# Layer 0's output projection with half its inputs by pairs of rows

## What is computed

```
y = jnp.concatenate([ya * jax.nn.silu(ga), yb * jax.nn.silu(gb)], axis=-1)
return y @ w_out            # layer 0: (1024 x 2048) @ (2048 x 1024)
...
x = x + gate[:, None, :] * y
```

## Time and profile before

| | |
|---|---|
| median of 3 runs | 1289.84 us (1289.24 to 1289.9) |
| the profiled execution | 1291.17 us |
| its span | 1289.4 us |
| TensorE busy | 1269.2 us, 98% |
| VectorE, ScalarE, GpSimd busy | 984.4, 641.3, 320.2 us |
| DMA | 167.31 MB, mean 130 GB/s |

### The profile page before, as it was taken

One profiled execution on the slowest core, in us unless ns is written; L12 is line 12 of the kernel. 1 busy time (PEld: TensorE's weight loads), 2 busy tenths in 40 slices (PEclk: granted clock), 3 DMA queues, 4 the chain that ended last, 5 costly groups with the idle time before them and its releaser, 6 DMA issues.

```text
span 1289.4 us, 15493 instructions
## 1 busy us (share of the span) xinstructions
PE 1269.2 (98%) x5655; PEld 1047.7 (81%) x5655; DVE 984.4 (76%) x1148; ACT 641.3 (50%) x904; POOL 320.2 (25%) x187
## 2 busy tenths in 40 slices
PE   7999999999999999999999999999999999999997
PEld 6877888888888888888888888888888888888886
DVE  5899997878878886868467599848748747797677
ACT  7456656465646464635558464234233333443353
POOL 1043443433424343000000013132223121413200
PEclk8999999999999999999999999999999999999999
DMA  9712232323242332597847302232232232782053
GB/s 303 210 49 70 84 118 86 104 81 114 65 120 70 114 107 74 172 386 268 305 155 271 113 17 66 69 96 65 68 96 67 66 98 82 287 284 65 18 179 132
DMA packets 151507, 167.31 MB, mean 130 GB/s; under 512 B 6342, under 2 KB 125318, under 8 KB 151432
## 3 DMA queue, kind: packets, MB, share of 16 engines
q1 hardware_dynamic: 151432, 166.33, 40.2%
HBM read 141.14 MB, written 25.17 MB: 129 GB/s over the span
## 4 chain that ended last, share of the span: by engine, by line
PE 86%; DVE 10%; SPq 2%; issue 2%; DMA 1%; ACT 0%; DVEq 0%; ACTq 0%
PE psum L2401 28%; PE psum L2403 28%; PE psum L2402 28%; DVE w_lo L1546 1%; DVE X L2320 1%; SPq L631 1%; DVE whole_x L2003 1%; DVE X L1636 1%; DVE y_lo L1613 1%; PE psum L2548 1%; DMA late<-in_mod_w 1%; SPq L644 0%; SPq L620 0%; DVE bufs L1785 0%; DVE w_lo L1568 0%
## 5 line engine op out<-in xcount | busy, mean ns | idle before, releaser
L2401 PE MATMUL psum<-X,w_hi 128*128 128x512 f32 x1252 | 490.3, 392 | 1.8 <-DVE w_lo L1546 0.9
L2402 PE MATMUL psum<-X,w_hi 128*128 128x512 f32 x1252 | 488.4, 390 | 0.0
L2403 PE MATMUL psum<-X,w_lo 128*128 128x512 f32 x1252 | 488.1, 390 | 0.0
L2401 PEld LDWEIGHTS psum<-X,w_hi 128*128 128x128 f32 x1252 | 235.7, 188 | 53.1 <-issue 2.7
L2403 PEld LDWEIGHTS psum<-X,w_lo 128*128 128x128 f32 x1252 | 235.7, 188 | 49.3
L2402 PEld LDWEIGHTS psum<-X,w_hi 128*128 128x128 f32 x1252 | 235.8, 188 | 48.9 <-issue 0.2
L999 ACT ACTIVATE w_hi<-ssum 128x512 fp32r<-128x512 f32 x156 | 97.1, 626 | 143.4 <-PE psum L2403 111.7
L1546 DVE TENSOR_TENSOR w_lo<-raw,w_hi 128x1024 fp32r<-128x1024 f32 x82 | 102.9, 1256 | 79.1 <-ACT w_hi L977 78.8
L928 POOL TENSOR_TENSOR ssum<-raw 128x512 f32<-128x512 f32 x39 | 73.6, 1886 | 311.2 <-DMA raw<-in_pool_w_in 253.1
L1568 DVE TENSOR_TENSOR w_lo<-ssum,w_hi 128x512 fp32r<-128x512 f32 x156 | 131.2, 849 | 25.6 <-ACT w_hi L999 25.0
L936 POOL TENSOR_TENSOR ssum<-ssum,raw 128x512 f32<-128x512 f32 x39 | 61.3, 1571 | 340.5 <-DVE w_lo L1568 340.5
(11 more groups left out here) (277 smaller groups left out, 1996.2 us busy)
## 6 DMA issues: line engine op xcount, KB each, us to landing
raw<-in_hy_w_in SPq DMA_DIRECT2D x48, 512.0 KB, 5.2
raw<-in_hy_w_out SPq DMA_DIRECT2D x48, 512.0 KB, 5.0
raw<-in_pool_w_in SPq DMA_DIRECT2D x32, 512.0 KB, 5.1
aux<-in_mod_w SPq DMA_DIRECT2D x16, 512.0 KB, 4.0
y_dram<-bufs SPq DMA_DIRECT2D x16, 512.0 KB, 2.9
raw<-in_mod_w SPq DMA_DIRECT2D x16, 512.0 KB, 5.2
y_dram<-gb_ SPq DMA_DIRECT2D x16, 512.0 KB, 3.3
raw<-in_pool_w_out SPq DMA_DIRECT2D x16, 512.0 KB, 6.0
```

The lines of the kernel that those rows point to most:

```text
L2401: nc.tensor.matmul(out_, whi, xhi, start=first, stop=False, skip_group_check=check)
L2402: nc.tensor.matmul(out_, whi, xlo, start=False, stop=False, skip_group_check=check)
L2403: return nc.tensor.matmul(out_, wlo, xhi, start=False, stop=last, skip_group_check=check)
```

## The change

Layer 0's output projection gets the form that layer 1's has. Input blocks 0 to 7 go by passes of 8 steps, A over rows 0 to 3, B over 4 and 5, C over 6 and 7. Input blocks 8 to 15 go by four pairs of row blocks ("O0"), between passes A and B. The other edits follow from it:

- the weights of blocks 8 to 15 are loaded into whole_x in pass A by `out_weights(0, kp)`, and GpSimd, VectorE and ScalarE make and split their T sums there;
- the 16 loads of the modulation leave the ring; each now goes to one of two rows of bufs (`mod_rows`), and the additions stand between the pairs' instructions on VectorE (`MODS_OF`: 4, 5, 5, 2 in the four pairs);
- y of passes B and C is loaded, 256 columns wide, to other places (`y_narrow`), as are the rows of x and their products with the gate;
- the gate's sums come behind product 7 of the first pair, the column sums in four pieces between the four parts of step 1 of pass B; the turns are groups of four, two and two row blocks;
- GpSimd starts its first T sums of layer 0 when the operand "ga" is split.

```diff
 PAIRS = [(name, i) for i in range(1, HEADS) for name in "ABC"]
+PAIRS += [("O0", j) for j in range(SB // 2)]
 PAIRS += [(name, n) for n in range(GROUPS) for name in ("V01", "G01", "V23", "G23") if n or name[1] == "2"]
-PAIRS += [("O", j) for j in range(SB // 2)]
+PAIRS += [("O1", j) for j in range(SB // 2)]
...
-N_STEPS = (2 * KB, KB)
-BLOCKS = {(0, "A"): (0, 1, 2), (0, "B"): (3, 4, 5), (0, "C"): (6, 7), (1, "A"): (0, 1, 2, 3), (1, "B"): (4, 5, 6, 7)}
+N_STEPS = (KB, KB)
+BLOCKS = {(0, "A"): (0, 1, 2, 3), (0, "B"): (4, 5), (0, "C"): (6, 7), (1, "A"): (0, 1, 2, 3), (1, "B"): (4, 5, 6, 7)}
...
+MODS_OF = (range(0, 4), range(4, 9), range(9, 14), range(14, 16))
...
+            def mod_load(m):
+                if m < 2:
+                    sp.wait_ge(ylo_done, KB)
+                else:
+                    sp.wait_ge(mod_done, m - 1)
+                _, chunk, kk = mods1[m]
+                sp.dma_start(mod_rows(m), mod_w[1][kk * P:(kk + 1) * P, chunk * D:(chunk + 1) * D])\
+                  .then_inc(mod_in[m % 2], 16)
+            def out_weights(layer, kp):
+                sp.wait_ge(full_of["4"], OUT[layer])
...
+            for n, step in enumerate(s for s in STEPS if s[:2] == (0, "A")):
                 ring_load(("W",) + step)
                 y_load(step)
+                if n in (1, 2):
+                    for kp in (2 * n - 2, 2 * n - 1):
+                        out_weights(0, kp)
+                if n in (3, 4):
+                    spill_head(HEADS - 1, n - 3)
+                if n >= 4:
+                    rows_load(0, n - 4)
+            for k in PAIRED[0]:
+                sp.wait_ge(y_out[k], 16)
+            o0 = OUT[0]
+            pair_load(o0)
+            pair_load(o0 + 1)
+            bias_load(1)
+            for m in (0, 1):
+                mod_load(m)
+            for b in (4, 5):
+                rows_load(0, b)
+            for m in (2, 3):
+                mod_load(m)
...
-            pool.wait_ge(h_ready, KB)
+            pool.wait_ge(lo_done, HI["ga", 0])
...
+            for n in range(3, KB):
+                step_splits(steps_a[n])
+                if n >= 4:
+                    low_out(0, n - 4)
+                if n < 7:
+                    t2_and_t4_out(0, n - 3)
...
+            for j, q in enumerate(OUT_PAIRS[0]):
+                mods = list(MODS_OF[j])
+                if j:
+                    take_22(q - 1)
+                    prep(q, 0)
...
+                add_11(q)
+                for m in mods[:2] if j < 3 else ():
+                    add_mod(m)
+                prep(q, 4)
+                for m in mods[2:4] if j < 3 else ():
+                    add_mod(m)
+                prep(q, 5)
...
+                add_12(q)
+                for m in mods[4:] if j < 3 else ():
+                    add_mod(m)
+                prep(q, 6)
```

More of the change, by code:

```diff
@@ L216, in build @@
         for n, (_, p, k) in enumerate(s for s in STEPS if s[0] == layer):
-            if (layer, p, k) == (1, "B", GROUP_ORDER[0]):
-                for q in range(OUT, len(PAIRS)):
+            if p == "B" and n == KB:
+                for q in OUT_PAIRS[layer]:
                     add_pair(q)
@@ L424, in build @@
         gate_in = sem("gate_in")
+        mod_in = [sem(f"mod_in{n}") for n in range(2)]
         y_out = [sem(f"y_out{k}") for k in range(2 * KB)]
@@ new lines, in _ @@
+            rows_store(1)
+            for m in (7, 8):
+                mod_load(m)
+            pair_load(o0 + 3)
+            for m in (9, 10):
+                mod_load(m)
+            rows_store(2)
+            mod_load(11)
+            rows_store(3)
+            rows_load(0, 7)
+            for m in (12, 13):
+                mod_load(m)
+            for step in STEPS[KB:KB + 2]:
+                ring_load(("W",) + step)
+            for m in (14, 15):
+                mod_load(m)
+            rows_load(0, 6)
@@ L818, in _ @@
+            for n, step in enumerate(s for s in STEPS if s[0] == 0 and s[1] != "A"):
+                if n >= 2:
+                    ring_load(("W",) + step)
+                y_load(step)
+                if n in (KB + 3, KB + 4):
+                    rows_store(n - KB + 1)
             for name in ("V0", "V1", "G0", "G1"):
@@ L1342, in _, with upper_out @@
-            passes(0, 3)
+                half = first // HALF
+                cols = slice(first - half * HALF, last - half * HALF)
+                nc.scalar.activation(h_half(k, half, 0)[:, cols], hx(k)[:, first:last], ACT.Copy)\
+                  .then_inc(hhi_ready, 1)
+            def upper_out(layer, kp):
+                at = 2 * ((2 * layer + 1) * KP + kp) + 2
+                act.wait_ge(t24_added, at)
+                act.wait_ge(t13_added, at)
+                for blocks in (slice(0, 4), slice(4, 7)):
+                    nc.scalar.activation(X[:, kp, blocks, 0, :], whole_x[kp][:, blocks, 1, :], ACT.Copy).then_inc(out_hi, 1)
@@ L1997, in residual @@
                     at = o_count(layer, b, half)
-                    if (layer, half) == (0, 0) and b >= 4:
-                        dve.wait_ge(*full(("T", b // 4 - 1 if b < 7 else 1, KB - 1)))
                     if (layer, b, half) == (1, 0, 0):
@@ L2108, in _ @@
             inverse(0, 7)
+            for k in range(KB):
+                low_h1(1, k)
             for k in range(KB):
@@ new lines, in _ @@
+                if p == "B":
+                    first = OUT[layer]
+                    for q in OUT_PAIRS[layer]:
+                        pair(q, after_1=(lambda: last_of(q - 1)) if q > first else None,
+                             after_7=gate_sums if q == OUT[0] else None)
+                for n, y_step in enumerate(y_steps[:ends]):
+                    if (layer, p, n) == (0, "A", 0):
+                        operands(y_step)
+                        for b, half in ((0, 0), (0, 1), (1, 0), (1, 1), (2, 0)):
+                            part_of(y_step, b, half)
+                        last_of(Q["C", HEADS - 1])
+                        part_of(y_step, 2, 1)
+                        operands(y_steps[1])
+                        for half in range(2):
+                            part_of(y_steps[1], 0, half)
+                        for half in range(2):
+                            part_of(y_step, 3, half)
+                        continue
+                    if (layer, p, n) != (0, "A", 1):
+                        operands(y_step)
+                    for b in blocks[1:] if (layer, p, n) == (0, "A", 1) else blocks:
+                        for half in range(2):
+                            if p == "B" and (n, b, half) == (0, 5, 1):
+                                last_of(OUT_PAIRS[layer][-1])
@@ L2787, in _ @@
                             part_of(y_step, b, half)
+                            if (layer, p, n) == (0, "B", 1):
+                                sums_between(2 * blocks.index(b) + half)
                     behind(layer, p, n)
```

610 lines of the change are left out of this document (319 added, 291 removed).

## The result

The changed kernel takes **1320.6 us** (median; 1319.3 to 1322.9), the kernel before, on the same chip, 1290.2: ratio **1.0233**, 95% interval 1.0221 to 1.0245. It is slower by 30.4 us, where 18.0 were forecast and the range ended at 1317. The sign was right, the size too small. The profiled execution took 1322.9 us (span 1321.1); before it was 1291.17 (span 1289.4).

The account below looks back on a forecast made before the run. TensorE, busy 98% of the span, was taken to bound the kernel, if operands arrive. Terms: -13.4 saved, +18.3 +1.6 in pass A, +9.9 +1.6 in the pairs: +18.0 on 1289.84, so 1307.8 us; range 1294 to 1317.

Parts of the forecast that it names:

- Clock behind the column sums, 1.6 us: Modulation sums in four pieces: the clock holds for the eight matmuls behind them, 1.6 us saved.
- GpSimd's start, 0.9 us: Layer 0's first GpSimd sums start one operand split later, so TensorE's wait for that split shortens: 0.9 us saved.
- Pass A, loads: Output-weight loads queue ahead of steps 2 and 3; step 3's weights land at T+19.2, T being product 4's end.
- Rival (a): Pass A's load queue is faster than layer 1's: step 3's weights at T+16.8, 2.4 us earlier, time 1305.4; chance 0.12.
- Pass A, chain and clock, 18.3 + 1.6: VectorE's fixed order of work makes step 7 late: 18.3 us lost, plus 1.6 for slow clock behind the last wait.
- The 8 us of the bound: Pass A's lower bound: with loads for nothing, VectorE's chain starts near 538.5 and still ends 8 us late.
- rival (c): Faster: step 3's operands come earliest, pass A loses only 8 us and the pairs nothing, 1284.4; chance 0.07.
- Pairs, 9.9 + 1.6 us: Product 4 waits for VectorE in the second and third pairs: 9.9 us lost, plus 1.6 for the clock.
- Passes B and C, 0: ScalarE and VectorE keep up with the 2.72 us steps, cover about 0.4 us a step: nothing lost.
- Rival (d): VectorE worse off: GpSimd contention in every pair, 5.2 us loads, slow clock behind four waits; +30, 1320; chance 0.09.
- Rival (b): Only pass A waits; in the pairs the additions' loads land in time as VectorE catches up: 1296.3; chance 0.22.
- Under 13 us of waits: Sign of being wrong: TensorE's waits between 526 and V0's start sum to under 13 us.

Follow-up runs that it names:

- run 6: The kernel before with only the column sums cut into four pieces between parts of step 6 of pass B: 1289.5 us, ratio 0.9988.
- run 7: The changed kernel with GpSimd's first sums of layer 0 starting again as in the kernel before: 1320.5 us.
- run 1: The changed kernel with the eight output-weight loads issued behind the loads of steps 2 and 3 instead of ahead: 1315.95 us, ratio 1.0203.
- run 2: The changed kernel loading only the first two of sixteen modulation rows, with all sixteen additions kept: 1308.4 us.
- run 3: The changed kernel loading only two modulation rows, and with fourteen of sixteen additions cut to 16 of 1024 columns: 1301.6 us.
- Run 5: The changed kernel with matmuls of a zero matrix filling TensorE's waits in pass A and the pairs: 1320.8 us, ratio 1.0232.
- run 8: The changed kernel with output-weight loads later, additions respaced 4, 5, 4, 3, GpSimd's first-pair sums delayed, its old start restored, norms apart: 1312.9 us.

## Why the prediction was right in sign and too small

By its own steps, in spans; the stages add up to what is missing (1.1 + 1.6 + 8.5 + 2.6 = 13.8 of 31.7 - 18.0 = 13.7):

- **48 matmuls, 10.9 us:** right. 48 fewer stand on the page, and layer 1 is unchanged.
- **Clock behind the column sums, 1.6 us:** right; run 6 measured 1.55 (0.5 to 2.7).
- **GpSimd's start, 0.9 us:** wrong. The wait moved from 71 to 96 us, and pass A begins 0.2 us later rather than 0.9 earlier: 1.1 us missing. The profiles of the runs, with the same work up to there but for GpSimd's start, have pass A begin between 525.5 and 528.3, so its start alone cannot show 0.9 us; the two waits of run 7 do. The step took a wait's end for a gain without asking who is late next.
- **Pass A, loads:** right. The weights of step 3 had landed at 551.1, where ScalarE's wait for them ends; product 4 ended at 532.9, so at T+18.2 (forecast T+19.2).

```profile
551.13 1.06 ACT L1048 ACTIVATE w_hi<-raw 128x1024 fp32r<-128x1024 f32 x1 [2.95 <-DMA raw<-in_hy_w_out]
```

By the estimate from the Trainium skill (DMA: Bandwidth & Descriptors, "Anatomy of one DMA") it would have been T+14.6; the measurement is 3.6 us later. The section gives that sum for one transfer issued by GpSimd, and here eleven were queued by SyncE, which the prediction did not say. Rival (a), T+16.8, is 1.4 us off, the forecast 1.0 the other way.
- **Pass A, chain and clock, 18.3 + 1.6:** nearly right. Measured, the pass ends at 594.6 instead of 592.8 (1.6 more from its own start). The 2.1 us of GpSimd's sums on top of VectorE's chain are the term left out.
- **The 8 us of the bound and of rival (c):** this does not follow from the prediction's own terms. From 538.5, its chain of 24.4 us would end at 562.9, where step 7 is needed at 562.7, and nearly nothing would be lost; 8 us would be lost from a start at 546.3, with the weights of step 3 at T+9, not T+12. Neither came near: with the loads moved (run 1) pass A still ended at 590.8 instead of the unhindered 572.9.
- **Pairs, 9.9 + 1.6 us:** this is the step that failed: the overlap of VectorE with TensorE in the pairs. From the start of the pairs to the last product 4 of layer 0 it took 97.9 us (689.73 - 594.57 + 2.72 for the last product), not 89.4. The sum looked at one deadline, product 4, in the second and third pair, and said that the fourth loses nothing. What the runs showed: VectorE, 26.8 and 27.1 us a pair (forecast 25.8 and 24.8), never catches up; through `add_rows` and ScalarE's snapshot it also holds product 3, and in the fourth pair too, until 684.2. In the first pair its additions waited 1.9 us twice, which I had not counted, and the loads landed in 4.7 us, not 4.0. Of this stage 11 to 12 us are waits for landings (run 2) and 7 to 8 the additions (run 3).
- **Slow clock:** I charged 1.6 twice. The trace has far more of it (0.93 over the pairs): the stage is 20.0 us longer than its 77.9 us of matmuls and sums, and TensorE's waits in it are only 12.7 of that; most of the other 7.3 is the lower clock. Added up on TensorE alone, the clock would seem to be most of the miss. Run 5 shows that in pass A it hides behind VectorE; in the pairs the distances of `take_22`, set by VectorE's work and waits, say the same.
- **Passes B and C, 0:** 2.6 us. I named the cover, 0.4 us a step of ScalarE, and costed its loss at nothing. Three waits of 0.9, 0.5 and 1.1 us came, the first because ScalarE split y only after its copy of the last pair's product 4 (`take_21`), and the other two at the end of pass C, where ScalarE was 44 of 60 us busy; their cause was not settled (run 8's guess, the norms, was wrong).
- **Tail, 0:** right.

Rival (d), 1320, had the right size and a part of the right cause: VectorE worse off than computed and loads near 5 us. It had 0.09. Rival (b) asked whether VectorE catches up in the pairs; it does not. "Under 13 us of waits" would have refuted the forecast; there were 31. The sign was not luck: pass A alone, by the mechanism forecast, lost more than the 12.5 us saved. The real fault is of form: the prediction summed TensorE's waits, one by one. Once one other engine is late at every one of them, the stage costs about what that engine's own work and waits add up to, and TensorE's waits are only where this shows.

## To carry to other kernels

When the busiest engine begins to wait for the same other engine at several places in a row, stop adding its waits: lay the other engine's work end to end, from the point where it is first late to the point where it is next idle, with its waits for loads inside. A quick test is to reorder that work: if the waits move and the time stays (here 11 us of pass A against 0 in the end), the other engine sets the pace. And work that was free in one stage is not free in another: the sixteen additions, which in the kernel before waited 0.6 us for their loads beside a VectorE with slack, cost 19 us (runs 2 and 3) with two rows of buffer on the engine that had become the bound. A scheme that gives TensorE fewer products needs its operand work to fit too.

## What the runs showed of the hardware

- Beside GpSimd's sums an operation of VectorE with both inputs in SBUF took 1.67 us instead of 0.69 (128x512) and 2.29 instead of 1.22 (128x1024). Moving a load earlier can lengthen other work by this: in run 1 about half of the expected gain went there.
- The granted clock fell to the lower of its two levels behind TensorE's waits of 6.6, 5.8, 2.5, 3.1 and 4.9 us (at 547, 582, 630, 643 and 670), where matmuls then took 0.63 us instead of 0.39 in the timeline. Matmuls of zeros in the waits kept it up behind four of the five (0.74 to 1.00 between 575 and 595); it fell behind other waits instead, and the time stayed.
- Thirty-two matmuls of one column in one piece were followed by the lower clock (0.86 over 12 us), four pieces of eight were not (1.00).
